# The long products' moving operand read as two halves in turns in a two-layer fp32 trunk on one core

## Time and profile before

| | |
|---|---|
| median of 3 runs | 2122.86 us (2122.51 to 2123.09) |
| profiled execution, own time | 2122.69 us |
| its span, first to last instruction | 2120.7 us |
| TensorE products busy | 2111.2 us, 9448 instructions |
| VectorE busy | 1481.2 us (70%), 1924 instructions |
| ScalarE busy | 1028.1 us (48%), 1180 instructions |
| GpSimd busy | 20.1 us |
| HBM read | 403.41 MB, 191 GB/s over the span |

### The profile page before, as it was taken

How to read it: one execution, slowest core, us unless ns; L and a number is a source line. 1 busy time by engine, 2 the same in 40 slices (tenths; PEclk the granted TensorE clock), 3 DMA queues, 4 the chain that set the end, 5 groups by cost and what they waited for, 6 DMA issues and landing times.

```text
span 2120.7 us, 25442 instructions
## 1 busy us (share of the span) xinstructions
PE 2111.2 (100%) x9448; PEld 1748.5 (82%) x9448; DVE 1481.2 (70%) x1924; ACT 1028.1 (48%) x1180; POOL 20.1 (1%) x24
## 2 busy tenths in 40 slices
PE   9999999999999999999999999999999999999998
PEld 7888888888888888888888888888888888888886
DVE  6797867764774775586778778577746855764875
ACT  6444346543543453454645554665434544544553
POOL 0000001000000000000000000000000000000000
PEclk9999999999999999999999999999999999999999
DMA  9655555656656656655555555456556566656553
GB/s 323 207 179 171 191 193 170 206 195 187 195 199 190 186 198 218 184 193 198 178 179 178 179 178 199 160 160 216 199 186 192 180 213 182 198 197 214 183 199 119
DMA packets 204077, 406.81 MB, mean 192 GB/s; under 512 B 6544, under 2 KB 9936, under 8 KB 203472
## 3 DMA queue, kind: packets, MB, share of 16 engines
q1 hardware_dynamic: 203712, 405.37, 58.3%
q10 hardware_dynamic: 272, 0.16, 0.0%
HBM read 403.41 MB, written 2.10 MB: 191 GB/s over the span
## 4 chain that ended last, share of the span: by engine, by line
PE 99%; DVE 0%; DVEq 0%; ACT 0%; issue 0%; POOL 0%; POOLq 0%
PE ps L1203 99%; PE ps L1352 1%; DVE x_sb L767 0%; PE ps L1431 0%; DVE act_pair L1111 0%; DVE act_pair L773 0%; ACT tmp L497 0%; DVE y_sb L1081 0%; DVEq L110 0%; DVE w_lo L800 0%; PE ps L1257 0%; POOL rs_bc L350 0%; PE ps L1545 0%; PE ps L1550 0%; DVE rst L856 0%
## 5 line engine op out<-in xcount | busy, mean ns | idle before, releaser
L723 DVE TENSOR_TENSOR w_lo<-w_raw,w_hi 128x1024 fp32r<-128x1024 f32 x750 | 910.7, 1225 | 561.9 <-ACT w_hi L394 558.2
L394 ACT ACTIVATE w_hi<-w_raw 128x1024 fp32r<-128x1024 f32 x750 | 789.9, 1061 | 897.0 <-PE ps L1203 893.2
L1203 PE MATMUL ps<-w_hi,act_pair 128*128 128x512 f32 x3456 | 1072.0, 390 | 0.4 <-ACT w_hi L457 0.3
L1203 PEld LDWEIGHTS ps<-w_hi,act_pair 128*128 128x128 f32 x3456 | 647.1, 188 | 136.2 <-issue 2.0
L1203 PE MATMUL ps<-w_lo,act_pair 128*128 128x512 f32 x1728 | 670.2, 390 | 0.0
L1203 PE MATMUL ps<-w_hi,hid_hi 128*128 128x512 f32 x1280 | 498.7, 390 | 0.0
L1203 PE MATMUL ps<-w_hi,hid_lo 128*128 128x512 f32 x1280 | 498.0, 389 | 0.0
L1203 PE MATMUL ps<-w_lo,hid_hi 128*128 128x512 f32 x1280 | 498.0, 389 | 0.0
L1203 PEld LDWEIGHTS ps<-w_lo,act_pair 128*128 128x128 f32 x1728 | 324.1, 188 | 66.6 <-DVE w_lo L800 0.4
L829 DVE STREAM_TRANSPOSE qT<-kT 32x256 f32<-32x256 f32 x608 | 265.0, 436 | 42.2 <-ACT kT L605 32.8
L1203 PEld LDWEIGHTS ps<-w_hi,hid_lo 128*128 128x128 f32 x1280 | 240.2, 188 | 50.0
(11 more groups left out here) (104 smaller groups left out, 474.3 us busy)
## 6 DMA issues: line engine op xcount, KB each, us to landing
w_raw<-in_ffn_w_dram SPq DMA_DIRECT2D x256, 1024.0 KB, 5.3
w_raw<-in_sb_w_in_dram SPq DMA_DIRECT2D x48, 1024.0 KB, 5.1
w_raw<-in_ab_w_in_dram SPq DMA_DIRECT2D x36, 1024.0 KB, 5.2
w_raw<-in_ab_w_out_dram SPq DMA_DIRECT2D x16, 1024.0 KB, 5.0
w_raw<-in_sb_w_out_dram SPq DMA_DIRECT2D x16, 1024.0 KB, 5.0
w_raw<-in_ab_w_in_dram SPq DMA_DIRECT2D x6, 512.0 KB, 8.5
x_sb<-in_x_dram SPq DMA_DIRECT2D x8, 256.0 KB, 7.2
gpost<-in_norm_post_mix_dram SPq DMA_DIRECT2D x2, 1024.0 KB, 7.9
```

The costliest lines, as they stand in the source:

```text
L394: nc.scalar.activation(w_hi[:, t % RING, :, :], w_raw[:, t // 2, h:h + 2, :], ACT.Copy).then_inc(hi_ready, 1)
L723: nc.vector.tensor_tensor(w_lo[:, t % RING, :, :], w_raw[:, t // 2, h:h + 2, :], w_hi[:, t % RING, :, :].bitcast(F32), ALU.subtract).then_ ...
L1203: return nc.tensor.matmul(dst, lhsT, rhs, start=start, stop=stop, skip_group_check=True)
```

## The change

Three access patterns are changed. Let a row of 512 columns have two halves of 256.

- The long products read the moving operand's row as column 0 of the first half, column 0 of the second half, column 1 of the first half, and so on (`halves`, `mm_w`). The output's 512 columns are written in a row as before.
- The stored order of `w_hi` and `w_lo` is changed to match: raw column 2c goes to position c, raw column 2c + 1 to position 256 + c (`in_halves`, `by_parity`). So the k-th column that a product reads is raw column k, and the results stand where they stood.
- ScalarE's and VectorE's conversions go over the raw weights in a row and write to the two halves in turns; VectorE reads `w_hi` in turns too.

The number of instructions, the waits, the transfers and the sizes of the tensors are the same. The hunks left out below make the same replacement of `mm` by `mm_w` in `first_ticks` (`products`), `opening_ticks`, `block0_hi` and `block0_lo`, and in `closing_ticks`. The suffix sums, the scores, the values and the transposes keep their patterns.

```diff
@@ -165,6 +165,13 @@
         junk_x = zs[:, 0:HG, :].rearrange("p h c -> p (h c)")
         gated = [junk[:, i * 512:(i + 1) * 512].rearrange("p (g t) -> p g t", t=T) for i in (1, 2)]
         lng_b, lnb_b = gpost[:, 0:A_W], gpost[:, A_W:D]
+
+        def by_parity(raw):
+
+            return raw.rearrange("p k (c h) -> p k c h", h=2)
+
+        def in_halves(w):
+            return w.rearrange("p k (h c) -> p k c h", h=2)
 
         def bank2(b):
             return ps[:, 2 * b:2 * b + 2, :]
@@ -391,7 +398,7 @@
                 if not (isinstance(u, int) and 8 * u + t < RING):
                     act.wait_ge(pe_ticks, 8 * u + (t - RING + 1))
                 h = 2 * (t % 2)
-                nc.scalar.activation(w_hi[:, t % RING, :, :], w_raw[:, t // 2, h:h + 2, :], ACT.Copy
+                nc.scalar.activation(in_halves(w_hi[:, t % RING, :, :]), by_parity(w_raw[:, t // 2, h:h + 2, :]), ACT.Copy
                                      ).then_inc(hi_ready, 1)
 
             def conv_at(u, t):
@@ -454,7 +461,9 @@
 
                 def first_kt(kt, landed, done):
                     act.wait_ge(landed, 16)
-                    nc.scalar.activation(w_hi[:, kt // 2, kt % 2, :], w_raw[:, 0, kt, :], ACT.Copy).then_inc(done, 1)
+                    i = kt % 2
+                    nc.scalar.activation(in_halves(w_hi[:, kt // 2, i:i + 1, :]), by_parity(w_raw[:, 0, kt:kt + 1, :]), ACT.Copy
+                                         ).then_inc(done, 1)
 
                 first_kt(0, s_kt[0], s_kt_hi)
                 first_kt(1, s_kt[1], hi_ready)
@@ -720,8 +729,8 @@
 
                 dve.wait_ge(hi_ready, 8 * u + (t + 1))
                 h = 2 * (t % 2)
-                nc.vector.tensor_tensor(w_lo[:, t % RING, :, :], w_raw[:, t // 2, h:h + 2, :],
-                                        w_hi[:, t % RING, :, :].bitcast(F32), ALU.subtract).then_inc(lo_ready, 1)
+                nc.vector.tensor_tensor(in_halves(w_lo[:, t % RING, :, :]), by_parity(w_raw[:, t // 2, h:h + 2, :]),
+                                        in_halves(w_hi[:, t % RING, :, :].bitcast(F32)), ALU.subtract).then_inc(lo_ready, 1)
 
             def conv_at(u, t):
                 if t < 4:
@@ -797,8 +806,10 @@
 
                 def first_kt(kt, converted, n, done):
                     dve.wait_ge(converted, n)
-                    nc.vector.tensor_tensor(w_lo[:, kt // 2, kt % 2, :], w_raw[:, 0, kt, :],
-                                            w_hi[:, kt // 2, kt % 2, :].bitcast(F32), ALU.subtract).then_inc(done, 1)
+                    i = kt % 2
+                    nc.vector.tensor_tensor(in_halves(w_lo[:, kt // 2, i:i + 1, :]), by_parity(w_raw[:, 0, kt:kt + 1, :]),
+                                            in_halves(w_hi[:, kt // 2, i:i + 1, :].bitcast(F32)), ALU.subtract
+                                            ).then_inc(done, 1)
 
                 first_kt(0, s_kt_hi, 1, s_kt_lo)
                 evacuate(0, 0)
@@ -1202,6 +1213,13 @@
             def mm(dst, lhsT, rhs, start, stop):
                 return nc.tensor.matmul(dst, lhsT, rhs, start=start, stop=stop, skip_group_check=True)
 
+            def halves(cols):
+
+                return cols.rearrange("p (h c) -> p c h", h=2)
+
+            def mm_w(dst, lhsT, w, start, stop):
+                return mm(dst, lhsT, halves(w), start, stop)
+
             def tick_tokens(buf, s, slot, hi, lo, ready, hi_done=(), opens=True):
 
                 pe.wait_ge(lo_ready, ready)
@@ -1210,9 +1228,9 @@
                     for b in range(TB):
                         dst, tok = ps[:, 2 * buf + b, :], slice(b * P, (b + 1) * P)
                         if b not in hi_done:
-                            mm(dst, hi[:, kt, tok], w_hi[:, slot, i, :], opens and kt == 0, False)
-                        mm(dst, hi[:, kt, tok], w_lo[:, slot, i, :], False, False)
-                        last = mm(dst, lo[:, kt, tok], w_hi[:, slot, i, :], False, kt == KT - 1)
+                            mm_w(dst, hi[:, kt, tok], w_hi[:, slot, i, :], opens and kt == 0, False)
+                        mm_w(dst, hi[:, kt, tok], w_lo[:, slot, i, :], False, False)
+                        last = mm_w(dst, lo[:, kt, tok], w_hi[:, slot, i, :], False, kt == KT - 1)
                 last.then_inc(pe_ticks, 1)
 
             def closing_ticks(buf, u, k):
...
```

More of the change, by code:

```diff
@@ L1231, in closing_ticks @@
                             dst, tok, slot = ps[:, 2 * buf + b, :], slice(b * P, (b + 1) * P), s % RING
-                            mm(dst, hid_hi[:, kt, tok], w_hi[:, slot, i, :], False, False)
-                            mm(dst, hid_hi[:, kt, tok], w_lo[:, slot, i, :], False, False)
-                            last = mm(dst, hid_lo[:, kt, tok], w_hi[:, slot, i, :], False, kt == KT - 1)
+                            mm_w(dst, hid_hi[:, kt, tok], w_hi[:, slot, i, :], False, False)
+                            mm_w(dst, hid_hi[:, kt, tok], w_lo[:, slot, i, :], False, False)
+                            last = mm_w(dst, hid_lo[:, kt, tok], w_hi[:, slot, i, :], False, kt == KT - 1)
                         if b == 1:
@@ L1243, in products @@
                     for b in range(TB):
-                        last = mm(ps[:, b, :], act[:, 2 * s + i, b * P:(b + 1) * P], w[:, s, i, :],
+                        last = mm_w(ps[:, b, :], act[:, 2 * s + i, b * P:(b + 1) * P], w[:, s, i, :],
                                   s == 0 and i == 0 and act is act_hi and w is w_hi, False)
@@ L1307, in opening_ticks @@
                     for i in range(2):
-                        mm(ps[:, 2 * buf + 1, :], act_hi[:, 2 * s + i, P:T], w_hi[:, s, i, :], s == 0 and i == 0, False)
+                        mm_w(ps[:, 2 * buf + 1, :], act_hi[:, 2 * s + i, P:T], w_hi[:, s, i, :], s == 0 and i == 0, False)
                 pe.wait_ge(lo_ready, 8 * u + 1)
@@ L1311, in opening_ticks @@
                 for i in range(2):
-                    mm(ps[:, 2 * buf + 1, :], act_hi[:, i, P:T], w_lo[:, 0, i, :], False, False)
-                    last = mm(ps[:, 2 * buf + 1, :], act_lo[:, i, P:T], w_hi[:, 0, i, :], False, False)
+                    mm_w(ps[:, 2 * buf + 1, :], act_hi[:, i, P:T], w_lo[:, 0, i, :], False, False)
+                    last = mm_w(ps[:, 2 * buf + 1, :], act_lo[:, i, P:T], w_hi[:, 0, i, :], False, False)
                 last.then_inc(pe_ticks, 1)
@@ L1317, in opening_ticks @@
                     for b in range(TB):
-                        mm(ps[:, 2 * buf + b, :], act_hi[:, 2 + i, b * P:(b + 1) * P], w_lo[:, 1, i, :], False, False)
+                        mm_w(ps[:, 2 * buf + b, :], act_hi[:, 2 + i, b * P:(b + 1) * P], w_lo[:, 1, i, :], False, False)
                 late_transposes(k, 1)
@@ L1322, in opening_ticks @@
                     for b in range(TB):
-                        last = mm(ps[:, 2 * buf + b, :], act_lo[:, 2 + i, b * P:(b + 1) * P], w_hi[:, 1, i, :], False, False)
+                        last = mm_w(ps[:, 2 * buf + b, :], act_lo[:, 2 + i, b * P:(b + 1) * P], w_hi[:, 1, i, :], False, False)
                 last.then_inc(pe_ticks, 1)
@@ L1362, in block0_hi @@
                     for i in range(2):
-                        mm(ps[:, 0, :], act_hi[:, 2 * s + i, 0:P], w_hi[:, s, i, :], s == 0 and i == 0, False)
+                        mm_w(ps[:, 0, :], act_hi[:, 2 * s + i, 0:P], w_hi[:, s, i, :], s == 0 and i == 0, False)
                 pe.wait_ge(post_done, u - 1)
@@ L1396, in block0_lo @@
                 for i in range(2):
-                    mm(ps[:, 0, :], act[:, i, 0:P], w[:, 0, i, :], False, False)
+                    mm_w(ps[:, 0, :], act[:, i, 0:P], w[:, 0, i, :], False, False)
             def late_transposes(k, s):
```

## The result

The changed kernel takes 2338.14 us (median of 4 runs, 2336.13 to 2340.25) against 2122.82 us: a ratio of 1.1014, 95% interval 1.0995 to 1.1034. The profiled execution took 2336.56 us with a span of 2334.5 us. It is 10% slower, inside the stated range and on the other side of the forecast.

A forecast was written before the change was run, and what follows sets the result against it. TensorE's long products were taken to bound the kernel: 2122.7 us, less 91 for faster products, plus 3 given back to VectorE, conversions at nothing, makes 2035 us. The range was 1990 to 2400 us.

The forecast's parts named there:

- Part (1): TensorE's 9024 long products reading in turns: 216.6 ns each instead of 226.7, saving 91 us.
- The 3.3 ns from the transposes: TensorE's time per transpose over the scores' pace, added to 213.3 ns as the loss left in each long product.
- 3 had been given back: 3 us returned because VectorE's fullest unit in layer 0, with 21.04 us of work, outlasts a unit shrunk to 20.8 us.
- Its 2025 us: Kernel time by the skill's 518 cycles, 215.8 ns a long product on TensorE, a saving of 98 us.
- Part (3): VectorE's 750 subtractions writing and reading the high part in turns: no cost taken; at worst 1092 ns more each.
- the end of the cover: VectorE's 4.05 us idle in an up unit is used up when a subtraction takes 1730 ns.
- The bound from above: VectorE's subtraction at one more time for each element: 2317 ns instead of 1225.
- Part (2): ScalarE's 750 conversions writing in turns: no cost taken, at worst 1973 ns each, hidden in an up unit's idle time.
- Rival (B): VectorE's conversions slow to 2317 ns, adding 255 us across the four stages: 2378 us; chance 0.15, 0.04 more if mild.
- Rival (A): TensorE's read in turns costs a second cycle per column: 1760 us more, 3880 us in all; chance 0.20.
- Rival (C): TensorE unchanged, loss from weight exchange (suffix sums) or order-blind reader, writes hidden: 2122.7 us; chance 0.11 including patterns cancelling.
- (D): The two patterns fall together to the old row by row order, so nothing changes; chance within the no-change rival's 0.11.

The follow-up runs named there:

- experiment 2: Kernel before the change with only the products' read in turns, conversions as before, output columns permuted: 2032.6 us.
- experiment 10: Kernel before with only the products' read order changed, to 0, 4, 1, 5, 2, 6, 3, 7 within every eight columns: 2032.6 us.
- 6: Kernel before with only the products' read changed, to every second column of a row, first the even then the odd: 4145.28 us.
- experiment 7: Kernel before with only VectorE's subtraction writing w_lo in turns, its reads in a row: 2261.56 us.
- experiment 4: Changed kernel with halves in turns by four columns (16 bytes), in products and conversions' writes alike: 2330.82 us, ratio 1.0979 to the kernel before.
- experiment 9: Kernel before with only ScalarE's conversion writing in turns: 2189.92 us.
- experiment 3: Kernel before with only the conversions' writes in turns, products reading in a row: 2378.4 us.
- experiment 11: Kernel before with only the products' read changed, to four quarters of 128 columns in turns: 2620.68 us.

## Why the prediction was right or wrong

**Part (1), the products, was right.** It put a product at 216.6 ns and the kernel, with conversions at no cost, at 2035 us. The runs gave 215.8 ns and 2032.6 us (experiment 2). The argument was that the loss sits in reading at full rate, as the fp32 scores lose nothing. Its conclusion held; the reason given, that two places are each asked half as often, didn't quite: by experiment 10 the two places may be 16 bytes apart, and by 6 a wrong step at the same rate doubles the time. The 3.3 ns from the transposes came out near what is left over 213.3 ns, 2.5 ns. That the total came within 3 us is in part luck: at 215.8 ns the saving would have been 98 us and not 91, and 8 us of it were lost elsewhere where 3 had been given back. The sentence on the Trainium skill ("TensorE: Matmul & The Clock Gate", Back-to-back issue gap) had 215.8 ns, and in the new order the trace agrees with it to the digit. (Its 2025 us leaves out the 3 us given back: 2028.) The same section of the Trainium skill gives this figure for a product by itself and about 131 ns for a stream of pairs of weight load and product; these products are such a stream, and no run here came under 215.8 ns.

**Part (3), VectorE's subtractions taken at nothing, is the step that failed.** "No row shows VectorE slower for its pattern" was true, but no row showed it writing single elements apart either, and absence of a row was read as absence of a cost. The measured mean is 2207 ns (2047 alone, experiment 7), over the 1730 ns that the same part had worked out as the end of the cover. Its write alone made the kernel 139 us slower. The bound from above, 2317 ns, was near and would have given the right sign. The Trainium skill's rule ("Advanced Engine Details and Errata", SBUF Cachelines: another 16-byte line at each access is penalised) stood in the prediction against the change. For the writes the runs bear the rule out, and experiment 4 adds that four elements a piece cost nothing. For TensorE's read they go against it: another 16 bytes at each column was the fastest order (experiments 2 and 10).

**Part (2), ScalarE's conversions hidden, failed as well.** The price, 1973 ns at most, was a little low (2091 alone, 2263 in the changed kernel). The cover was checked in an up unit only, 18.8 of 21.76 us; in layer 1 it was 17.36 + 8.2 us, over the unit, which the windows of before would have shown. And in the up unit itself the idle time did not cover it all, since part of it is waiting for VectorE in a fixed order. Worth 67 us by experiment 9.

**Rival (B) was what happened.** Its time, 2378 us, is that of the conversions alone (2378.4 us, experiment 3). Its parts were less exact than the sum: by the same bounds of stages, that run lost 66 us in the first MLP where half of 150 was priced, 52 in layer 0's mixer for 59, and 68 in layer 1's for 46; the last also holds ScalarE's part (30.7 us when alone, experiment 9). What it left out is that the products' gain comes on top, in the down units above all: 2338 instead of 2378 us. It got 0.15 where (A) got 0.20.

**Rival (A) was wrong for this pattern** and near in its price for another: 451 ns a product and 4145 us, for its 422 ns and 3880 us, when every second column is read. **Rival (C)**, with the suffix sums as its witness, was wrong too; those sums read in pieces with gaps, which was the objection noted beside them. (D) is excluded by the change of both rates.

## What to carry to other kernels

A change of layout has a reader and a writer, and each engine has its own rule for what is cheap; price both, in the fullest unit of each engine and not in a typical one. Idle time is cover only where the engine does not spend it waiting, in a fixed order, for another engine that becomes slower too. Where no row shows a pattern, its cost is open, and the side with the thinner cover decides the sign. And where a permutation pays for the reader of one memory, look for the place where undoing it is free: here the reads from PSUM, some 170 instructions, instead of 1500 writes to SBUF.

## What the runs showed of the hardware that was not expected

- The time of an fp32r product of 512 columns, each with its own weight load, depends on the order in which the moving operand is read: 215.8 ns (518 cycles) for two halves in turns or for 0, 4, 1, 5 within eight columns, 226.7 in a row, 250 for fours in turns, 283 for quarters in turns, 328 to 333 for pairs in turns (output in pairs too), 451 for every second column. An explanation that fits the order of most of these is two paths in turn, each of which reads 16 bytes at a time (argued, not shown): a path then uses four columns of a piece (215.8), two (226.7 and 250) or one (283, 333, 451). It foretold experiment 10 and missed the size of experiment 11; why one column a piece costs so differently stays open. The Trainium skill ("SBUF — State Buffer", Specifications) asks for two hits on a 16-byte line for full bandwidth; in a row each path would have two and is still 5% slower.
- Writing single fp32 elements to two places in turns takes ScalarE from 1061 to 2091 ns for 1024 elements and VectorE from 1225 to 2047; four at a time costs nothing. Reading 8 bytes apart, writing in a row, gave 1563 and 1513 ns. Reading two far places in turns cost VectorE 46 ns.
- With both engines writing in turns, two others suffered. ScalarE's relu, which reads PSUM and writes in a row, had a mean of 1501 ns (676 before), and not in the runs with only one of them in turns (668 and 675). And GpSimd's small power of two columns, which has a mean of 1.35 us in the kernel before, took 12.95 us beside seven subtractions end to end. First that, then the same operation in experiment 7, where VectorE alone wrote in turns:

```profile
1596.79 14.88 DVE L732 TENSOR_TENSOR w_lo<-w_raw,w_hi 128x1024 fp32r<-128x1024 f32 x7
...
1596.96 12.95 POOL L371 TENSOR_TENSOR rst<-rst,neg_half 128x2 f32<-128x2 f32 x1 [17.17 <-DVE rst L830]
...
1532.71 2.24 POOL L371 TENSOR_TENSOR rst<-rst,neg_half 128x2 f32<-128x2 f32 x1 [16.72 <-DVE rst L833]
```

The Trainium skill ("SBUF — State Buffer", SBUF: two separate sides) describes a port pair that a VectorE operation with two SBUF inputs holds for the whole instruction against a GpSimd operation that reads SBUF. One subtraction (2.0 us) of waiting is in keeping with the 2.24 us, which ran beside six subtractions end to end (1532.54 to 1544.01 us); the 12.95 us are more than that rule gives. Like the slow relu they were seen only where both engines wrote in turns; no run took that apart.
